# Attention probabilities turned by VectorE and by transfers through DRAM instead of by TensorE

## The reference

```python
h = rmsnorm_2(x, norm_g[l])
proj = h @ w_in[l]
q, k, v, za, u, vs, zs, gm = jnp.split(proj, IN_SPLITS_2, axis=-1)
q = partial_rope(q.reshape(B, S, ATT_HEADS, HEAD_DIM), pos)
a = window_sink_attention(q, k, v, att_sinks[l])
a = (a * jax.nn.silu(za)) @ w_att_out[l]
# inside window_sink_attention, for each chunk of 64 queries and the 192 keys that it sees:
m = jnp.maximum(jnp.max(s, axis=-1, keepdims=True), sink)
p = jnp.exp(s - m)
denom = jnp.sum(p, axis=-1, keepdims=True) + jnp.exp(sink - m)
o = jnp.einsum('bhgnqk,bnkhd->bnqhgd', p / denom, vb.astype(jnp.float32))
```

## Time and profile before

| what | value |
|---|---|
| median of 3 runs | 1270.48 us (1270.28 to 1270.49) |
| profiled execution | 1270.71 us, span 1268.9 us |
| TensorE busy | 1261.5 us, 99% of the span |
| VectorE busy | 893.3 us, 70% |
| ScalarE busy | 619.7 us, 49% |
| GpSimd busy | 724.1 us, 57% |

### The profile page before, as it was taken

The page is one execution under the profiler, slowest core; times in us unless marked ns, Lnnn a source line. Parts: engine busy times, 40 slices in busy tenths (PEclk is TensorE's granted clock), DMA queues, the critical chain, the costliest instruction groups (busy, mean ns, idle before and its releaser), DMA issues.

```text
span 1268.9 us, 19753 instructions
## 1 busy us (share of the span) xinstructions
PE 1261.5 (99%) x7542; PEld 1091.2 (86%) x7542; DVE 893.3 (70%) x1380; ACT 619.7 (49%) x989; POOL 724.1 (57%) x513
## 2 busy tenths in 40 slices
PE   9999999999999999999999999999999999999998
PEld 7877877777888899989988998877778899999886
DVE  6775555777444599558855869766656999998587
ACT  6123533565334555325522546354556656666454
POOL 3543433434543588658865866444333786666767
PEclk9999999999999999999999999999999999999999
DMA  7253176564423335353535335333522233225351
GB/s 225 87 150 108 42 199 159 144 187 125 124 75 100 100 100 166 100 166 100 167 101 166 103 106 174 108 88 88 137 67 68 76 121 100 89 83 199 100 210 73
DMA packets 205371, 154.89 MB, mean 122 GB/s; under 512 B 67488, under 2 KB 194976, under 8 KB 204512
## 3 DMA queue, kind: packets, MB, share of 16 engines
q1 hardware_dynamic: 204800, 153.06, 40.3%
q10 hardware_dynamic: 480, 0.59, 0.1%
HBM read 136.20 MB, written 14.16 MB: 118 GB/s over the span
## 4 chain that ended last, share of the span: by engine, by line
PE 96%; ACT 1%; DVE 1%; DMA 1%; POOL 1%; issue 0%; SPq 0%; ACTq 0%
PE gemm L961 16%; PE gemm L962 16%; PE gemm L969 16%; PE gemm L1235 10%; PE gemm L1234 10%; PE gemm L1239 10%; PE gemm L985 2%; PE gemm L986 2%; PE gemm L991 2%; PE gemm L1018 2%; PE gemm L1019 2%; PE gemm L1024 2%; PE mix L1355 1%; PE mix L1343 1%; PE mix L1332 1%; DMA raw<-w_in 1%
## 5 line engine op out<-in xcount | busy, mean ns | idle before, releaser
L793 POOL TENSOR_TENSOR wlo<-raw,whi 128x512 fp32r<-128x512 f32 x264 | 368.7, 1428 | 288.6 <-ACT whi L1491 269.1
L961 PE MATMUL gemm<-hh,whi 128*128 128x512 f32 x544 | 215.3, 396 | 0.2 <-ACT whi L1491 0.2
L962 PE MATMUL gemm<-hl,whi 128*128 128x512 f32 x544 | 212.4, 390 | 0.0
L813 POOL TENSOR_TENSOR wlo<-raw,whi 128x512 fp32r<-128x512 f32 x108 | 159.4, 1501 | 40.5 <-ACT whi L1685 32.4
L1491 ACT ACTIVATE whi<-raw 128x2048 fp32r<-128x2048 f32 x62 | 118.4, 1909 | 46.0 <-PE gemm L969 19.8
L969 PE MATMUL gemm<-hh,wlo 128*128 128x512 f32 x544 | 136.0, 391 | 0.0
L1234 PE MATMUL gemm<-hh,whi 128*128 128x256 f32 x496 | 124.8, 284 | 0.0
L961 PEld LDWEIGHTS gemm<-hh,whi 128*128 128x128 f32 x544 | 102.1, 188 | 26.3 <-issue 4.3
L1235 PE MATMUL gemm<-hl,whi 128*128 128x256 f32 x496 | 124.4, 284 | 0.0
L962 PEld LDWEIGHTS gemm<-hl,whi 128*128 128x128 f32 x544 | 102.3, 188 | 20.4
L969 PEld LDWEIGHTS gemm<-hh,wlo 128*128 128x128 f32 x544 | 101.7, 188 | 20.9
(11 more groups left out here) (545 smaller groups left out, 3124.6 us busy)
## 6 DMA issues: line engine op xcount, KB each, us to landing
raw<-w_in SPq DMA_DIRECT2D x53, 1024.0 KB, 5.3
raw<-w_gu SPq DMA_DIRECT2D x44, 512.0 KB, 5.2
raw<-w_down SPq DMA_DIRECT2D x16, 512.0 KB, 4.4
p_rows<-p_blocks SPq DMA_DIRECT2D x32, 160.0 KB, 3.2
p_t<-p_rows SPq DMA_DIRECT2D x8, 640.0 KB, 4.0
raw<-w_o SPq DMA_DIRECT2D x5, 1024.0 KB, 5.2
raw_b<-w_branch SPq DMA_DIRECT2D x16, 256.0 KB, 6.8
blk_b<-w_o SPq DMA_DIRECT2D x8, 512.0 KB, 7.1
```

The lines of the kernel that those rows point to most:

```text
L793: last = nc.gpsimd.tensor_tensor(a(wlo), a(raw), as_f32(a(whi)), ALU.subtract)
L813: return nc.gpsimd.tensor_tensor(part_of(wlo, u, b), raw_block(u, f, k), as_f32(part_of(whi, u, b)), sub)
L961: mm(bank[:, :], w, xh[:, k, :], start=(k == 0), stop=False)
L962: mm(bank[:, :], w, xl[:, k, :], start=False, stop=False)
```

## The change

For the first twelve pairs (steps 0 to 23) TensorE no longer turns and ScalarE no longer copies. Behind the scaling of a pair VectorE turns it in 32x32 blocks into `w_blocks` (two buffers), SyncE writes that to `w_rows` in DRAM with four stores of 128 KB in pieces of 128 bytes (`store_probs`), waits until they have landed, and loads 512 KB back into `w_turned_p` (`load_probs`, two buffers). `w_values` reads from there and stands a slot later, in the odd slots 5 to 27 (slot 2v + 5 for pair v). Pairs 12 to 15 are as before. SyncE's loops are written out in one order by hand. Three small rows (`lng`, `lnb`, `bsb`), whose place in SBUF the new buffers take, are loaded after pair 11 and not before this stage; the first reader waits for them.

```diff
+        w_blocks = [place(f"w_blocks{i}", [P, 1024], Z0 + at) for i, at in enumerate((80, 98))]
+        w_turned_p = [place(f"w_turned_p{i}", [P, 1024], Z0 + 68 + 4 * i) for i in range(2)]
...
+        BY_DMA = 12
+        S_PE = 2 * BY_DMA
...
+            def store_probs(v):
+
+                sp.wait_ge(sem("w_tb"), v + 1)
+                for f in range(4):
+                    sp.dma_start(w_rows[v % 2].rearrange("(j a) (k c) -> a k j c", a=32, c=P)[:, :, :, 32 * f:32 * f + 32],
+                                 w_blocks[v % 2][32 * f:32 * f + 32, :].rearrange("a (k j b) -> a k j b", j=4, b=32)).then_inc(sem("w_stored"), 16)
+
+            def load_probs(v):
+
+                sp.wait_ge(sem("w_stored"), 64 * (v + 1))
+                if v >= 2:
+                    sp.wait_ge(sem("w_v"), 2 * v - 2)
+                sp.dma_start(w_turned_p[v % 2][:, :], w_rows[v % 2]).then_inc(sem("w_in"), 16)
...
             load_wide(0)
+            store_probs(5)
+            load_probs(5)
+            store_probs(6)
+            load_probs(6)
             swap_rotary(3)
             store_turned(4)
+            load_wide(1)
+            store_probs(7)
+            store_turned(5)
+            load_probs(7)
+            load_wide(2)
+            store_probs(8)
+            store_turned(6)
+            load_probs(8)
+            load_wide(3)
+            store_turned(7)
+            for v in (9, 10):
+                store_probs(v)
+                load_probs(v)
+            slot_free(n_ao)
+            load(n_ao, cols(w_ao, 0, UC))
+            store_probs(11)
+            load_probs(11)
+            sp.wait_ge(sem("w_v"), S_PE)
+            sp.dma_start(lng[:, :], ln_g.partition_broadcast(P)).then_inc(sem("c2_in"), 16)
...
             def w_turn(s):
                 m, c = s // TT, s % TT
                 pe.wait_ge(sem("w_p"), s + 1)
-                if s >= 1:
-                    pe.wait_ge(sem("w_pt"), s)
+                if s > S_PE:
+                    pe.wait_ge(sem("w_pt"), s - S_PE)
...
             def w_values(s):
                 m, c = s // TT, s % TT
-                pe.wait_ge(sem("w_pt"), s + 1)
+                if s < S_PE:
+                    pe.wait_ge(sem("w_in"), 16 * (s // 2 + 1))
+                    turned = w_turned_p[s // 2 % 2][:, s % 2 * SEQ:s % 2 * SEQ + SEQ]
+                else:
+                    pe.wait_ge(sem("w_pt"), s - S_PE + 1)
+                    turned = wpt[:, s % 2, :]
...
-                    for s in (i - 4, i - 3):
-                        if 0 <= s < STEPS:
-                            w_values(s)
-                if 0 <= i - 2 < STEPS:
+                first = i - 4 if i % 2 == 0 else i - 5
+                if (S_PE <= first < STEPS) if i % 2 == 0 else (0 <= first < S_PE):
+                    w_values(first)
+                    w_values(first + 1)
+                if S_PE <= i - 2 < STEPS:
                     w_turn(i - 2)
...
+            def w_blockwise(v_):
+                dve.wait_ge(sem("w_p"), 2 * v_ + 2)
+                if v_ >= 2:
+                    dve.wait_ge(sem("w_stored"), 64 * (v_ - 1))
+                blocks = w_blocks[v_ % 2]
+                for s in (2 * v_, 2 * v_ + 1):
+                    own = blocks[:, s % 2 * SEQ:s % 2 * SEQ + SEQ]
+                    if s % TT == 0:
+                        for h in range(2):
+                            last = v.transpose(own[:, (2 * h + 1) * P:(2 * h + 2) * P], wp[:, s % 3, h, P:])
+                    else:
+                        last = v.transpose(own, wp[:, s % 3].rearrange("p h c -> p (h c)"))
+                last.then_inc(sem("w_tb"), 1)
```

More of the change, by code:

```diff
@@ L719, in store_turned @@
                                  x_turned[m % 4][32 * f:32 * f + 32, :].rearrange("a (j b) -> a j b", b=32)).then_inc(sem("x_stored"), 16)
[L721 to L734, removed]
@@ L736, in load_wide, with load_qz @@
+            def load_qz(n):
+                slot_free(n)
+                p, j = divmod(n - n_qz, 2)
+                load(n, cols(w_in2, (I2_ZA if j else I2_Q) + p * UC, UC))
             def load_wide(u):
+                slot_free(n_vs + u)
                 slot = raw[:, (n_vs + u) % 2].rearrange("p (k a) c -> p k (a c)", a=2)
                 load(n_vs + u, cols(w_in2, I2_VS + u // 2 * 512, 512, 4 * (u % 2), 4), slot)
+            load_qz(n_qz)
+            load_qz(n_qz + 1)
+            sp.wait_ge(sem("key_s"), 1)
@@ new lines, in _ @@
+            for a, b in ((0, 8), (8, 0)):
+                for kv in range(2):
+                    sp.dma_start(key_t[a:a + 8, kv, :], key_s[64 * kv + b:64 * kv + b + 8, :]).then_inc(sem("key_in"), 16)
+            load_qz(n_qz + 2)
+            swap_rotary(0)
+            load_qz(n_qz + 3)
+            load_qz(n_qz + 4)
+            store_probs(0)
+            swap_rotary(1)
+            load_probs(0)
+            store_turned(0)
+            load_qz(n_qz + 5)
+            store_probs(1)
+            store_turned(1)
@@ L740, in _ @@
+            load_probs(1)
+            load_qz(n_qz + 6)
+            store_probs(2)
+            load_probs(2)
+            store_probs(3)
+            load_probs(3)
+            swap_rotary(2)
+            store_turned(2)
+            load_qz(n_qz + 7)
+            store_probs(4)
+            store_turned(3)
+            load_probs(4)
             load_wide(0)
+            store_probs(5)
+            load_probs(5)
+            store_probs(6)
+            load_probs(6)
             swap_rotary(3)
@@ L743, in _ @@
+            sp.wait_ge(sem("w_v"), S_PE)
+            sp.dma_start(lng[:, :], ln_g.partition_broadcast(P)).then_inc(sem("c2_in"), 16)
+            sp.dma_start(lnb[:, :], ln_b.partition_broadcast(P)).then_inc(sem("c2_in"), 16)
+            sp.dma_start(bsb[:, :, :].rearrange("p g i -> p (g i)"), sg_b.partition_broadcast(P)).then_inc(sem("c2_in"), 16)
             for u in range(1, 4):
-                slot_free(n_vs + u)
-                load_wide(u)
-                store_turned(4 + u)
-            stream(n_ao, 4, both(tiles_of(w_ao, 0)))
+                slot_free(n_ao + u)
+                load(n_ao + u, cols(w_ao, u * UC, UC))
@@ L1835, in w_exp @@
                     s = 2 * v + e
-                    if s >= 3:
-                        act.wait_ge(sem("w_t"), s - 2)
+                    if s >= S_PE + 3:
+                        act.wait_ge(sem("w_t"), s - 2 - S_PE)
+                    elif s >= 3:
+                        act.wait_ge(sem("w_tb"), (s - 3) // 2 + 1)
                     for h in range(2):
@@ L1846, in w_turned @@
             def w_turned(s):
-                act.wait_ge(sem("w_t"), s + 1)
-                if s >= 2:
+                act.wait_ge(sem("w_t"), s + 1 - S_PE)
+                if s >= S_PE + 2:
                     act.wait_ge(sem("w_v"), s - 1)
@@ L2636, in _ @@
             T = tiles_before(n_e0)
-            dve.wait_ge(sem("c2_in"), 64)
+            dve.wait_ge(sem("c2_in"), 16)
             tile_ready(T)
@@ L2717, in w_slot @@
                         w_norm(i // 2)
+                    if i < S_PE:
+                        w_blockwise(i // 2)
                 if i % TT == 3 and i >= 7:
```

11 lines of the change are left out of this document (4 added, 7 removed).

## The result

The changed kernel takes 1281.5 us (median of 4 runs, 1280.93 to 1282.14) against 1270.45 (1270.28 to 1270.49): a ratio of 1.0088, 95% interval 1.0075 to 1.0100. It is slower by 11 us, and the prediction (1270.1, range 1266.4 to 1274.8) was wrong. The profiled execution took 1281.31 us, its span 1279.4, that is 10.5 more than before.

A forecast was written before the change was run, and what follows sets the result against it. TensorE, 99% busy, was taken as the bound: 6.4 us net leaves its queue, 6.1 us of waits for SyncE's trips return, leaving 0.4 us: 1270.7 - 0.4 = 1270.3, 1270.1 as a median, range 1266.4 to 1274.8.

The forecast's parts named there:

- What leaves TensorE's queue: Slots 2 to 25: removed turns free 11.0 us, 4.6 come back, net 6.4 us if no wait comes.
- the change of shape: First gemm product directly behind scores or products with v takes 0.43 us, not 0.23: 23 x 0.20 = 4.6 us.
- In the Q part I expect little waiting: SyncE's queue, Q part: six slots of two units hold two weight loads to three trips, with little waiting.
- The ledger of the wide part: SyncE's queue from wide unit 1's load: 894.0 plus 47.8 puts pair 11 in SBUF at 941.8; TensorE waits 6.1 us.
- slower: Slots 21 to 27: TensorE waits for landed pairs; four weight loads take 6.4 us, not 5.3, giving 1274.5; chance 0.26.
- The clock is 1.00 ... so it is no term: All profile windows show the 2.4 GHz level, so the clock adds nothing to the sum.
- is hidden: First wide unit: a wait of about 1 us (0 to 3.4) for VectorE, hidden by the queue's later waits.
- Faster: Trips shorter or beside the weights: 0.9 saved per trip ends the queue 4.5 us earlier, 1265.6; chance 0.24.
- lower end of 1266: Ledger start 2.7 earlier, or stores moving in 2.6 (1.5 less in five), gives 1266 to 1267.5.

The follow-up runs named there:

- the run with six pairs: Six pairs instead of twelve turned by VectorE and transfers, against the kernel with 1 KB pieces, turning moved and pair loads on ScalarE: 1275.97 us, ratio 1.0046.
- both edits: Changed kernel with pieces of 1 KB, VectorE's turning behind the next pair's maxima and a new order on SyncE's queue: 1275.92 us, ratio 1.0042.
- the last one: Pieces of 1 KB and turning moved, with SyncE's queue reordered again (pair loads ahead of x_turned stores, last weight load behind pair 9's trip): 1268.1 us, ratio 0.9983.

## Why the prediction was wrong

In one sum: I set waits of 6.1 us against work of 6.4, and there were 13.5 us of waits (4.5 in the Q part, where I expected little, 8.5 in the wide part in place of 6.1, 0.5 for GpSimd) and 3.4 us of lower clock, where I had none.

- **What leaves TensorE's queue: 6.4 us net.** Right. The run with neither turning nor trip took 1264.05 where the sum gave 1264.1; 11.0 of turns and 0.20 a time for the change of shape are together as sized, and the 0.43 of a first gemm product is in the chain of that run behind scores and products with v alike.
- **"In the Q part I expect little waiting".** This step failed first. The changed kernel waited 1.5 us at pair 2 and 3.0 at pair 4. I had counted three trips and two weight loads for six slots without adding them up. Of three trips two stand behind a weight load, and each held the queue for 9.2 us (mean) before its load could go out. From pair 1's first store (836.64) to pair 4's (868.62) the queue took 32.0 us, for what TensorE asks for in six slots of 4.6 us, 27.6 us.
- **The ledger of the wide part.** It was to begin at 894.0 and the load of unit 1 went out at 900.43: 6.4 us late, from the Q part (with neither turning nor trip it went out at 891.41). It then had 47.8 us and took about 52 (900.43 to 948.86, and 3.7 for the load's median landing): 941.8 became 952.5. The terms for a trip behind a load (4.7 and 1.4, measured 6.3 to 6.9) were nearly right, as was the landing of a pair's load (3.7 and 3.7); for one behind a weight load I took 4.7 + 2.8 = 7.5 and 9.2 was measured (8.3 to 10.2). The error was to add the moving of weights and of small pieces as if neither slowed the other, although showed x_turned stores landing after 5.1 us behind a weight load and 1.9 elsewhere; I put that under the rival "slower" and not in the sum.
- **"The clock is 1.00 ... so it is no term".** This failed too. It is no term only while nothing waits. Of six waits of 2.7 to 3.8 us, in the changed kernel and in the one with waits added, four were followed by the lower level, at 1.7 us a time, two of them in the changed kernel: 3.4 us of the 10.5.
- **VectorE "is hidden".** Right as far as the trips' waits hid all but 0.5 us of it, and wrong in what it meant. I expected about 1 us at the first wide unit; without the trip it was 3.2 there, 4.3 elsewhere and 1.7 by the clock. The 1.3 us a pair stand between one pair's scaling and the next pair's maxima, and a scaling of 1.0 us that took 4.96 beside GpSimd came on top; the runs do not divide the loss between the two.
- **The rivals.** "Faster" (1265.6) could not have come with this order of VectorE even with perfect trips: 1274.2 is what the change gives then. Nor was any trip of the changed kernel as short as that rival's 7.5 us: it took 6.3 to 10.2 to the load's issue and 3.7 more to the landing. "Slower" was the right side, and for the wide part it was right in mechanism and price: the four weight loads landed 5.6, 6.5, 6.3 and 6.4 us after issue instead of 5.3, and the stretch from unit 1's load to the landing of pair 11 took 4.3 us more than my sum, where this rival had 4.4. It ended at 1274.5 because it, too, began the ledger at 894.0 and had no term for the clock. The two limits that each cost 10 us or more were priced as additions of 1 to 4.
- **The range.** Its lower end of 1266 needs both of its terms at once; each by itself gives 1267.4 or 1268.6. It does not touch the miss, which is at the other end.

Open: why one wait of 2.7 us left the clock alone and two did not; the 2.5 us between profile and median in the run with six pairs; how much of VectorE's lateness is the collision with GpSimd and how much the 1.3 us a pair, since moving the turning took both away; how much of the waits with 1 KB pieces is the trip's own; whether the changed kernel's own order on SyncE's queue, with both edits, would do as well as the last one.

## What to carry to other kernels

When a stage has two engines or queues close to full, price each alone with the other perfect: here the trips alone cost 20.5 us and VectorE's turning alone 10.3, together 17.4, and the view of waits named only the one that came last. Extra work for an in-order engine belongs in the hole where it waits for another engine's answer, not between that answer's products and the next request; the same 1.3 us cost 10 us in one place and nothing in the other. Before a turn goes through DRAM, choose the layout that makes its pieces long: reading in runs of 32 columns cost nothing here, and an eighth of the pieces was worth 7 us. And then look at the order of the queue that carries it, since two orders of the same transfers were 7.8 us apart.

## What the runs showed of the hardware

- Issuing four stores of 1024 pieces of 128 bytes took 2.8 us with no other transfer, 3.9 behind a 512 KB load and 5.7 to 6.7 behind a 1 MB load, and on ScalarE's own queue 6.0 to 7.6 while a weight load moved. With pieces of 1 KB it took 1.8 us with nothing in front and 1.9 to 3.6 behind a weight load.
- VectorE's scaling of four 128x128 tiles took 1.0 us alone, 2.05 (kernel before) and 2.59 (neither turning nor trip) partly beside GpSimd's subtractions, and 4.96 wholly beside them (no trip).
- TensorE's products with v from runs of 32 columns, 256 apart, took 0.93 and 1.15 us a pair, as from contiguous columns (0.93 and 1.15).
- Two of three added waits of 2.7 us were followed by 8 us at a mean granted clock of about 0.79.
